# A down-projection in two decoder layers: residual rows by single tiles, four raw places in its last step, a product kept aside, and norm steps placed between groups

## What is computed

```
u = causal_dwconv(h @ w_up, conv_w, conv_b)      # h: normed x, 1024 x 1024; u: 1024 x 5632
gate, val = split(u, 2)
x = x + (silu(gate) * val) @ w_down              # 1024 x 2816  times  2816 x 1024
h_next = rms_norm(x, mix_norm[1])                # only after layer 0
```

## Time and profile before

| what | value |
|---|---|
| runs shown | 2541.0, 2546.72 and 2546.8 us, median 2546.72 us |
| the profiled execution's own time | 2542.37 us |
| its span, first to last instruction | 2540.6 us |
| mean granted TensorE clock | 0.984 |
| PE busy | 2436.7 us, 96% of the span |
| DVE busy | 1731.4 us, 68% |
| ACT busy | 1030.8 us, 41% |
| POOL busy | 194.6 us, 8% |
| DMA traffic | 257.72 MB, mean 101 GB/s |
| the down-projection in f0 | about 939 to 1198 us of the span |
| the down-projection in f1 | about 2304 to 2540 us of the span |

### The profile page before, as it was taken

One profiled execution on the slowest core, in us unless ns is written; L12 is line 12 of the kernel. 1 busy time (PEld: TensorE's weight loads), 2 busy tenths in 40 slices (PEclk: granted clock), 3 DMA queues, 4 the chain that ended last, 5 costly groups with the idle time before them and its releaser, 6 DMA issues. The chain is left out here.

```text
span 2540.6 us, 32368 instructions
## 1 busy us (share of the span) xinstructions
PE 2436.7 (96%) x11700; PEld 2056.7 (81%) x11700; DVE 1731.4 (68%) x2934; ACT 1030.8 (41%) x2118; POOL 194.6 (8%) x269
## 2 busy tenths in 40 slices
PE   7999979999999998998999999998999999999898
PEld 7998757888888886777889889887888888887777
DVE  4432564479998987885553562463769989988895
ACT  6433443344444443335434442333334444443332
POOL 1010121000000000001212022122000000000000
PEclk9999988999999999999999999999999999999999
DMA  4231112222222247643102011212532222227653
GB/s 147 89 88 22 48 70 58 84 68 83 92 83 75 91 154 273 228 138 128 55 17 80 34 34 42 59 34 80 173 107 83 83 75 92 83 85 256 250 176 140
DMA packets 207349, 257.72 MB, mean 101 GB/s; under 512 B 38184, under 2 KB 141592, under 8 KB 207192
## 3 DMA queue, kind: packets, MB, share of 16 engines
q1 hardware_dynamic: 203032, 255.65, 30.6%
q10 hardware_dynamic: 4160, 0.02, 0.1%
HBM read 206.54 MB, written 49.09 MB: 101 GB/s over the span
## 5 line engine op out<-in xcount | busy, mean ns | idle before, releaser
L52 PE MATMUL psum<-f_T_lo 128*128 128x512 f32 x616 | 246.8, 401 | 31.0 <-DVE f_T_lo L654 29.3
L53 PE MATMUL psum<-f_T_lo 128*128 128x512 f32 x616 | 242.2, 393 | 0.0
L54 PE MATMUL psum<-f_T_lo 128*128 128x512 f32 x616 | 241.8, 393 | 0.0
L52 PE MATMUL psum<-w_hi,hT_hi 128*128 128x512 f32 x576 | 229.3, 398 | 3.9 <-DVE w_lo L1415 2.2
L54 PE MATMUL psum<-w_hi,hT_lo 128*128 128x512 f32 x576 | 226.3, 393 | 0.0
L53 PE MATMUL psum<-w_lo,hT_hi 128*128 128x512 f32 x576 | 226.1, 393 | 0.0
L52 PEld LDWEIGHTS psum<-f_T_lo 128*128 128x128 f32 x616 | 117.0, 190 | 68.2 <-DVE f_T_lo L654 40.9
L52 PEld LDWEIGHTS psum<-w_hi,hT_hi 128*128 128x128 f32 x576 | 124.8, 217 | 22.1 <-issue 3.5
L54 PEld LDWEIGHTS psum<-w_hi,hT_lo 128*128 128x128 f32 x576 | 125.0, 217 | 17.8
L53 PEld LDWEIGHTS psum<-w_lo,hT_hi 128*128 128x128 f32 x576 | 125.1, 217 | 16.6
L52 PE MATMUL psum<-hT_hi,f_up_hi 128*128 128x512 f32 x352 | 137.4, 390 | 0.4 <-DVE f_up_lo L593 0.4
(11 more groups left out here) (412 smaller groups left out, 6053.1 us busy)
## 6 DMA issues: line engine op xcount, KB each, us to landing
raw<-in_ffn_w_up_dram SPq DMA_DIRECT2D x88, 512.0 KB, 4.7
activations<-f_act SPq DMA_DIRECT2D x44, 512.0 KB, 2.6
f_up_pieces<-activations SPq DMA_DIRECT2D x38, 512.0 KB, 4.1
w_raw<-in_b_w_in_dram SPq DMA_DIRECT2D x18, 1024.0 KB, 6.1
f_up_pieces<-in_ffn_w_down_dram SPq DMA_DIRECT2D x20, 512.0 KB, 4.9
x_between<-XY SPq DMA_DIRECT2D x16, 512.0 KB, 5.3
XY<-x_between SPq DMA_DIRECT2D x4, 2048.0 KB, 15.4
f_up_pieces<-activations SPq DMA_DIRECT2D x28, 256.0 KB, 3.9
```

Of the source, the lines that this page charges most:

```text
L52: nc.tensor.matmul(out, lhs_hi, rhs_hi, start=start, stop=False)
L53: nc.tensor.matmul(out, lhs_hi, rhs_lo, start=False, stop=False)
L54: return nc.tensor.matmul(out, lhs_lo, rhs_hi, start=False, stop=stop)
```

## The change

The waits follow new numbers of the semaphore `added`, since some additions are joined and some move.

- `load_rows(t)` loads one tile of 128 rows (512 KB). Tiles 4 to 7 are issued behind `load_down` of groups 5, 7, 9 and 10; tiles 0 to 3 behind groups 14, 16, 18 and 20. The store of the last activation slice moves from group 8 to group 12.
- The last taps move to behind `lows(3)` and `lows(6)`, the last gating product to behind `lows(8)`, its silu on ACT from group 4 to group 7.
- Pairs of DVE additions with a common operand become one instruction of 1024 elements a row, which reads that operand twice (`both`).
- Products 4 to 7 of step 1 are copied to `conv_out` by ACT (`keep_second`, before `high_parts(23)`) and added to the rows later (`rows_kept`, after groups 28 to 31). PE's products 4 to 7 of step 2 wait for the copies.
- Step 3 has four raw places in place of two, and `load_right` waits for groups further back.
- The norm steps of tiles 0 to 3 on ACT and DVE get another order among the groups of step 3; PE turns tile 3 one group later; the fifth tile is turned behind the tail.
- The low parts of the next layer's first weights move from DVE to POOL, and their high parts on ACT from group 23 to group 25.

```
-            return up.pieces[:, 2 * (n % 2), :]
+            return (up.pieces[:, 2, :], up.pieces[:, 6, :], up.room[:, 0, FIRST], up.pieces[:, 0, :])[(n - LAST) % 4]
...
+        p2_copy = [conv_out[i // 2][:, (i % 2) * HALF:(i % 2 + 1) * HALF] for i in range(4)]
...
             def load_right(g):
-                sp.wait_ge(b_split, parts_until(LAST + g - 1))
+                sp.wait_ge(b_split, parts_until(LAST + g - 3 if g >= 4 else LAST - 2 + max(0, g - 1)))
...
-            def load_rows(i):
+            def load_rows(t):
                 sp.wait_ge(p_done, ALL)
-                sp.dma_start(X[:, 4 * i:4 * i + 4, :], x_mid.rearrange("(t p) n -> p t n", p=P)[:, 4 * i:4 * i + 4, :]).then_inc(x_loaded[i], 16)
+                sp.dma_start(X[:, t, :], x_mid[t * P:(t + 1) * P, :]).then_inc(x_loaded[t // 4], 16)
...
                 load_down(n)
-                if n == 8:
+                if n in (5, 7, 9, 10):
+                    load_rows({5: 4, 7: 5, 9: 6, 10: 7}[n])
+                if n == PAIRS + 1:
                     store_act(FC - 1)
-                    for i in (1, 0):
-                        load_rows(i)
+                if n in (14, 16, 18, 20):
+                    load_rows((n - 14) // 2)
...
+            def keep_second():
+                act.wait_ge(prod_done, FC)
+                for i in range(4):
+                    act.wait_ge(out_done, 12 + i + 1)
+                    nc.scalar.activation(p2_copy[i], psum[:, 4 + i, :], ACT.Copy).then_inc(p2_copied, 1)
...
             for n in range(2, LAST):
+                if n == 2 * PAIRS + 1:
+                    keep_second()
                 high_parts(n)
-                if n == 4:
+                if n == 7:
                     silu(FC - 1)
...
-                if begin and n == 2 * PAIRS + 1:
+                if begin and n == 2 * PAIRS + 3:
...
-            for g in range(4):
+            for g in range(PAIRS):
+                if norm and g >= 4:
+                    if g == 4:
+                        square(0)
+                    if g == 5:
+                        scale(0)
+                        square(1)
+                    if g == 6:
+                        scale(1)
+                        norm.act_high(act, 0)
+                        square(2)
+                    if g == 7:
+                        scale(2)
+                    if g == 8:
+                        norm.act_high(act, 1)
+                        square(3)
+                    if g == 9:
+                        scale(3)
+                    if g == 10:
+                        norm.act_high(act, 2)
                 high_parts(LAST + g)
...
+                norm.act_high(act, 3)
                 act.wait_ge(b_split, parts_until(LAST + PAIRS))
...
+                square(4)
+                square(5)
+                scale(4)
+                scale(5)
+                square(6)
+                norm.act_high(act, 4)
+                scale(6)
...
             def second_sums():
                 for i in range(4):
                     dve.wait_ge(out_done, 8 + i + 1)
                     dve.wait_ge(added, X11A + 4)
-                    add(k1[:, i, :], k1[:, i, :], psum[:, i, :])
-                    add(k7[:, i, :], k7[:, i, :], psum[:, i, :])
-                for i in range(4):
-                    dve.wait_ge(out_done, 12 + i + 1)
-                    add(x11[i], x11[i], psum[:, 4 + i, :])
+                    k_both = halves(h_room[1][:, DH + i, :])
+                    add(k_both, k_both, both(psum[:, i, :]))
...
-                add(x21[i], x21[i], k7[:, i, :])
-                add(x22[i], x22[i], k7[:, i, :])
+                add(halves(X[:, i, :]), halves(X[:, i, :]), both(k7[:, i, :]))
...
+            def rows_kept(i):
+                dve.wait_ge(p2_copied, i + 1)
+                add(x11[i], x11[i], p2_copy[i])
...
             lows(2)
-            taps_of(FC - 1, 1)
             sums(4)
             lows(3)
-            taps_of(FC - 1, 0)
+            taps_of(FC - 1, 1)
...
                     lows(n)
-                if n == 5:
+                if n == 6:
+                    taps_of(FC - 1, 0)
+                if n == 8:
                     multiply(FC - 1)
...
-                if begin and n == 2 * PAIRS + 6:
-                    begin.low_parts(dve)
+                if 2 * PAIRS + 6 <= n < 2 * PAIRS + 10:
+                    rows_kept(n - 2 * PAIRS - 6)
...
+            for g in range(5, PAIRS):
+                lows(LAST + g)
+                if norm and g in (5, 7, 9):
+                    norm.dve_gain(dve, (g - 5) // 2)
+                elif norm:
+                    norm.dve_low(dve, (g - 6) // 2)
...
             def _(pool):
+                if begin:
+                    begin.low_parts(pool)
                 for t in range(TT):
                     norm.pool(pool, t)
...
+                elif step == 2 and which == 1:
+                    pe.wait_ge(p2_copied, i + 1)
...
-                if norm and 2 <= g < 6:
-                    turn_first(g - 2)
+                if norm and g in (2, 3, 4, 6):
+                    turn_first((2, 3, 4, 6).index(g))
...
-            self.nc.vector.tensor_tensor(self.lo[kh], self.raw(kh), self.hi[kh].bitcast(F32), ALU.subtract).then_inc(self.split, 1)
+            self.nc.gpsimd.tensor_tensor(self.lo[kh], self.raw(kh), self.hi[kh].bitcast(F32), ALU.subtract).then_inc(self.split, 1)
```

More of the change, by code:

```diff
@@ L441, in high_parts @@
                 if n >= LAST:
-                    act.wait_ge(e_loaded[n % 2], 16 * (g // 2 + 1))
+                    act.wait_ge(e_loaded[g % 4], 16 * (g // 4 + 1))
                     wait_group(act, n - 4 if g >= 4 else LAST - 2 + g // 2)
@@ L514, in _ @@
                 act.wait_ge(b_made, 3 * LAST)
-            for g in range(4):
+            for g in range(PAIRS):
[18 more added lines that the diff above has]
+                        norm.act_high(act, 2)
                 high_parts(LAST + g)
             if norm:
-                square(0)
-                scale(0)
-            high_parts(LAST + 4)
-            if norm:
-                square(1)
-                scale(1)
-            high_parts(LAST + 5)
-            for t in range(4):
-                if norm:
-                    norm.act_high(act, t)
-                    if t < 2:
-                        square(t + 2)
-                        scale(t + 2)
-                high_parts(LAST + 6 + t)
-            high_parts(LAST + PAIRS - 1)
-            if norm:
-                act.wait_ge(b_split, parts_until(LAST + PAIRS))
-                for t in range(TT // 2, TT):
-                    square(t)
-                    if t > TT // 2:
-                        norm.act_high(act, t - 1)
-                    scale(t)
-                norm.act_high(act, TT - 1)
+                norm.act_high(act, 3)
+                act.wait_ge(b_split, parts_until(LAST + PAIRS))
+                square(4)
[5 more added lines that the diff above has]
+                scale(6)
+                square(7)
+                norm.act_high(act, 5)
+                scale(7)
+                norm.act_high(act, 6)
+                norm.act_high(act, 7)
         @block.vector
@@ L665, in rows_first, with both, halves @@
             def rows_first(i):
-                dve.wait_ge(x_loaded[1], 16)
+                dve.wait_ge(x_loaded[1], 64)
                 add(x11[i], x11[i], k1[:, i, :])
+            def both(x):
+                return x.unsqueeze(1).broadcast_to([P, 2, HALF])
+            def halves(x):
+                return x.rearrange("p (h n) -> p h n", n=HALF)
             def second_sums():
@@ L693, in third_second @@
                 dve.wait_ge(out_done, 20 + i + 1)
-                add(x22[i], x22[i], psum[:, 4 + i, :])
-                add(x12[i], x12[i], psum[:, 4 + i, :])
+                pieces = X[:, i:i + 5:4, SECOND]
+                add(pieces, pieces, both(psum[:, 4 + i, :]))
             def rows_last(i):
-                dve.wait_ge(added, X2P + 8)
+                dve.wait_ge(added, X2P + 4)
                 dve.wait_ge(out_done, 24 + i + 1)
@@ L797, in _ @@
                 dve.wait_ge(act_stored, 16 * FC)
-                norm.dve_gain(dve, 0)
-            lows(LAST + 5)
-            for t in range(4):
-                if norm:
-                    norm.dve_low(dve, t)
-                    if t < 3:
-                        norm.dve_gain(dve, t + 1)
-                lows(LAST + 6 + t)
-            lows(LAST + PAIRS - 1)
-            for i in range(3):
+            for g in range(5, PAIRS):
[4 more added lines that the diff above has]
+                    norm.dve_low(dve, (g - 6) // 2)
+            if norm:
+                norm.dve_gain(dve, 3)
+            for i in range(4):
                 rows_last(i)
+                if norm and i == 1:
+                    norm.dve_low(dve, 3)
             if norm:
-                norm.dve_gain(dve, 4)
-            rows_last(3)
-            if norm:
-                norm.dve_low(dve, 4)
```

(13 more changed lines are left out.)

21 lines of the change are left out of this document (10 added, 11 removed).

## The result

The changed kernel takes 2521.25 us in the median (2519.33 to 2525.38, 4 runs). The kernel before took 2543.9 us beside it (2541.0 to 2546.8, 4 runs). The ratio is 0.9913, 95% interval [0.9899, 0.9928]. The forecast was 2512, with a range from 2498 to 2530. The profiled execution took 2521.81 us, its span is 2520.0.

The account below looks back on a forecast made before the run. PE was taken as the bound, with holes, the big one before group 8 from row loads ahead of needed sets. 11.0 + 11.0 - 1.3 + 2.5 + 6.2 + 1.5 = 30.9 us off 2542.4 gave 2511.5, stated as 2512; range 2498 to 2530.

Parts of the forecast that it names:

- step 0, layer 0: Down-projection groups 0 to 12, layer 0: of 13.5 us lost, 11.0 gained by moving the row loads (2.3 to 13.5).
- step 0, layer 1: Down-projection groups 0 to 12, layer 1: same code and same hole as layer 0, so 11.0 us gained.
- step 2, layer 0: Groups 22 to 33, layer 0: 1.3 us more lost, 3.4 gained from DVE's additions turning to 4.1 lost through POOL's subtractions.
- step 2, layer 1: Groups 22 to 33, layer 1, without next weights: 4.8 us lost today, 2.3 after, gain 2.5 (0 to 4.8).
- step 3, layer 0: Group 33 through the tail, layer 0: gain 6.2 us of 9.7 from four raw places and the new norm order.
- step 3, layer 1: End of layer 1: the 1.38 us wait before the tail goes with four raw places; gain 1.5 (0 to 1.5).
- The rival in which the rows are not the cause: The hole before group 8 stays, 22 us of the gain go: 2533.5 us; chance 0.06.
- the slower one: Sixteen single row tiles get in the way of sixteen sets, 12 us slower: 2554 us; chance 0.04.
- what stays late: Step 0, each layer: low parts still late before groups 4, 6, 7 and 9, 2.5 us with slow first matmuls.
- step 0 becomes bound by loads: Rival: delays don't heal before group 11, each layer keeps 7.5 of 13.5 us lost: 2521.5 us; chance 0.2.
- The lock: Layer 0, step 2: POOL's two subtractions hold DVE through a shared port, 4.7 us paid by PE in groups 25 and 26.
- The rival without a lock: POOL works beside DVE unhindered in step 2: 2507 us; chance 0.15.

Follow-up runs that it names:

- experiment 1: The kernel before with only the single row tiles and the later store of the last activation slice: 2526.84 us, ratio 0.9924.
- experiment 2: The changed kernel with the rows loaded again by two 2 MB transfers behind group 8, all else kept: 2534.23 us, ratio 0.9959.
- experiment 8: The changed kernel with all row tiles behind groups 11 to 14 and 16 to 19, the last activation store behind group 15: 2524.1 us, ratio 0.9925.
- experiment 9: The changed kernel, but from group 4 of step 0 each of a set's three loads is issued when its own place is free: 2511.9 us, ratio 0.988.
- experiment 3: The changed kernel with the low parts of the next weights back on DVE, behind group 28: 2515.33 us, ratio 0.9889.
- experiment 4: The changed kernel, low parts still on POOL, but ACT makes the next weights' high parts after group 32, not 25: 2517.03 us, ratio 0.9893.
- experiment 5: The changed kernel with two raw places in step 3 again instead of four: 2524.66 us, ratio 0.9922.
- experiment 6: The changed kernel, ACT taking tile 1's high part ahead of group 43's and tiles 2 and 3's behind it, DVE's order following: 2516.41 us, ratio 0.9883.
- experiment 7: The changed kernel with the last taps moved behind the low parts of group 2 and those of group 5: 2520.8 us, ratio 0.9904.

## Why the prediction was right in its cause and half too large in its gain

Forecast 30.9 us off the profiled execution, measured 20.6. The terms, one by one:

| term | forecast | measured |
|---|---|---|
| step 0, layer 0 | 11.0 | 8.1 |
| step 0, layer 1 | 11.0 | 8.6 |
| step 1, both layers | 0 | -0.6 |
| step 2, layer 0 | -1.3 | -0.8 |
| step 2, layer 1 | 2.5 | 3.0 |
| step 3, layer 0 | 6.2 | 4.8 |
| step 3, layer 1 | 1.5 | 1.7 |
| outside the down-projections | 0 | -4.2 |

- **The cause was right.** The rows made the hole (experiments 1 and 2), and the slow clock behind it went with it. The rival in which the rows are not the cause falls, and so does the slower one: without tiles in step 0 it is only 1.3 and 1.8 us shorter (experiment 8), and with them step 1 loses 0.5 and 0.1.
- **Step 0 was mis-sized, 5.3 us of the 10.3.** The term that was too small is what stays late: 2.5 us a layer in the forecast, 5.4 and 4.7 measured over the 65.4 of the earlier trace rows's rate. It rests on "6.6 us; then `sums` 1.8 and `lows` 2.3, so 10.7 us [...] against 10.9", a slack of 0.2, and the 6.6 is that of one set, the set of group 3. Where DVE waited for a later set in the changed kernel, it came later after its issue: set 4 after 7.9 us, set 7 after 7.2, set 9 after 7.6, set 10 after 6.9. So the ring (issue, landing, sums, low parts, next issue) took 12.1, 11.4, 11.8 and 11.2 us for two groups, not 10.7. Part of that is the tiles: with none in step 0 (experiment 8) sets 7 and 10 come after 6.5 us and DVE doesn't wait for set 9, but set 4 still takes 7.6. This is the rival "step 0 becomes bound by loads", in a milder form, between the 2.5 of the forecast and the rival's 7.5; its sign, long waits of `sums` for loads in groups 5 to 11, is there (3.15 us before `sums(7)`). It was given 0.2. Experiment 9 shows the ring, since step 0 gets shorter when parts of a set are issued earlier.
- **The lock: nearly the right price by a wrong course, and with luck.** I charged DVE 4.7 us in groups 25 and 26. DVE paid nothing there: POOL took 24 us more than alone, then held DVE, 2.88 us in one operation, at a moment when DVE was already late, and PE paid 2.58 and some 1.8 of restart in group 30. Experiments 3 and 4 put 3.0 and 3.5 us on it, and 1.6 of these are the fall of the clock: in experiments 5, 6, 8 and 9, which have the same lock without that fall, step 2 of layer 0 gains 0.8 to 1.3 us in place of losing 0.8. The rival without a lock falls too. My test "two POOL subtractions of 2.36 us" failed, "PE waiting 4 to 5 us around groups 25 and 26" was off by four groups and 2 us.
- **Step 2 of layer 1**, without next weights, gained 3.0 (2.5 forecast): joined additions and the kept product together do what was worked out. Experiment 1, which has neither, keeps the 64.6 us of before; what each of the two brings was not tried.
- **Step 3 of layer 0:** the chain gave waits of 0.9 and 2.3 us; there are 0.88 and 2.28, and one of 0.23. The 0.3 for restarts was too small: from 1160 to 1165 us the clock is 0.66. I had named a slow restart and not charged it; with its 1.5 us the term would have been right. In experiment 7, where the clock stays up behind the same wait, the stretch gains 6.4. Experiment 6 shows that the wait was a choice of order, not of work.
- **Step 3 of layer 1** is the four places, 1.7 (experiment 5).
- **Outside**, 4.2 us that I had at nothing. Half is where the next layer's first product meets its norm, most of it a fall of the clock that only the kernel before does not show; the other half is scatter of the kind that the stretches between show in all kernels. What makes the first half was not tried. Experiment 1 has 1.3 us of it with the norm of before. The wait itself, 0.5 us longer, is for POOL, which starts 12.3 us after its last work (10.3 before) without a releaser that the profile names.

## What to carry to other kernels

A prefetch that nobody is waiting for belongs behind the loads that somebody waits for, in pieces small enough that each of these meets one at most. Where places are reused in turn, work out the ring (issue, landing, work, place free) with the landing time of the busiest stretch, and issue each part of a set when its own place is free, not when the last one is. Before moving work to GpSimd, look for a gap of VectorE to put it in, and before a norm step on a shared engine, look at what is queued behind it. Before an edit is credited with a microsecond or two, look whether the clock fell in one of the two executions and not in the other.

## What was not expected of the hardware

- A GpSimd subtraction of two 128x1024 operands in memory, 2.36 us alone, took 26.6 us beside a VectorE that ran operations on such operands back to back. Six kernels of the experiments (2, 5 to 9) show the same, 26.57 to 26.61 us, and in each it ended where VectorE waited 0.9 to 1.9 us for a load. VectorE's own operations showed no delay until then; the one behind that wait took 0.95 to 1.93 us in place of 0.68, and the next one 2.88. PE's wait was 2.55 to 2.60 us in all seven, whether the load was 0.9 or 1.9 us late.
- A wait of PE of 2.3 to 2.6 us can make the granted clock fall, and need not. In the 5 us behind the wait before group 30 it is 0.66, a mean of the levels 1.2 and 2.4 GHz, in three kernels (the changed one, experiments 2 and 7), and 1.00 in four (5, 6, 8 and 9). It is 0.66 also behind the 2.28 at 1160.37; in experiment 7 the same 2.28 us stand at 1162.00 and the clock stays at 1.00, and its step 3 is 1.6 us shorter for that alone. What tells the two apart was not tried. Behind the waits of about 1 us in step 0 of the changed kernel it is 1.00 everywhere.

The window of the changed kernel, and that of experiment 7:

```profile
1160.00:1165.00 5.00, 4.63 (x13) 3.67 (x14) 3.27 (x4) 1.33 (x2) 0.00 (x0) 0.66 0.02 3
```

```profile
1160.00:1165.00 5.00, 3.00 (x13) 2.50 (x14) 4.11 (x5) 1.89 (x4) 0.00 (x0) 1.00 0.01 3
```
